# A decoder block in one program: the first 128 tokens go through attention, merge, projections and routing alone, and the second 128 go through them beside the first ones' expert gathers

## The reference

```python
mod = silu(c) @ ada_w + ada_b                    # 1024 x 6144: sh1, sc1, g1, sh2, sc2, g2
h = rms_norm(x, norm1_g) * (1 + sc1) + sh1
z = h @ w_in                                     # q, k, v of both attentions, indexer, gates
# NSA, 8 heads: compressed blocks + selected blocks + window, causal, gated by head
# DSA, 8 heads: the indexer picks 64 keys for each query, then softmax over them
merged = sigmoid(g_nsa) * (o_nsa @ w_br_nsa) + sigmoid(g_dsa) * (o_dsa @ w_br_dsa)
x = x + g1 * (merged @ w_out)
h = rms_norm(x, norm2_g) * (1 + sc2) + sh2
q = (h @ peer_wq).reshape(T, 8, 2, 64)           # routing: 8 heads, two halves each
s_half, i_half = top_k(einsum("thcd,hcnd->thcn", q, subkeys), 16)   # 128 keys a half
top_s, top_p = top_k(sums of the two halves, 16)                    # 16 of 16384 experts
act = gelu(einsum("cd,chkd->chk", h, u[eidx]))   # a row of 1024 of u for each token and pick
x = x + g2 * einsum("chk,chkd->cd", softmax(top_s) * act, v[eidx])  # and one of v
return rms_norm(x, final_g)
```

## Time and profile before

| | |
|---|---|
| median of 3 runs | 1091.7 us |
| the profiled execution's own time | 1091.95 us |
| its span, first to last instruction | 1089.7 us |
| mean granted TensorE clock | 0.915 |
| first gather issued | 406.4 us |
| HBM read over the span | 328.58 MB |

### The profile page before, as it was taken

The page is one execution under the profiler, slowest core; times in us unless marked ns, Lnnn a source line. Parts: engine busy times, 40 slices in busy tenths (PEclk is TensorE's granted clock), DMA queues, the critical chain, the costliest instruction groups (busy, mean ns, idle before and its releaser), DMA issues.

```text
span 1089.7 us, 8493 instructions
## 1 busy us (share of the span) xinstructions
PE 811.3 (74%) x2512; PEld 431.9 (40%) x2512; DVE 632.3 (58%) x1533; ACT 207.2 (19%) x529; POOL 501.2 (46%) x517
## 2 busy tenths in 40 slices
PE   2499889999999860067777777777777777777774
PEld 2344577878888750022222222222222222222221
DVE  4622346679331158998558559459549449545545
ACT  3001132333401240022112112112022022021200
POOL 1000000000000007777777777777777777777472
PEclk8599889986599895579999999999999999999998
DMA  9743304467315009999999999999999999999995
GB/s 340 290 143 100 142 1 149 174 219 252 135 44 208 0 23 381 380 410 409 409 409 409 409 409 409 409 410 409 410 409 409 410 409 410 409 409 410 340 399 215
DMA packets 103470, 330.20 MB, mean 303 GB/s; under 512 B 9025, under 2 KB 11265, under 8 KB 103425
## 3 DMA queue, kind: packets, MB, share of 16 engines
q0 software_dynamic: 73728, 268.47, 62.3%
q1 hardware_dynamic: 29248, 60.73, 15.7%
q10 hardware_dynamic: 448, 0.46, 0.1%
HBM read 328.58 MB, written 1.05 MB: 302 GB/s over the span
## 4 chain that ended last, share of the span: by engine, by line
PE 30%; POOL 27%; DMA 18%; issue 13%; DVE 11%; ACT 1%; DVEq 0%; SPq 0%; POOLq 0%; ACTq 0%
POOL arena L694 14%; POOL extra L683 9%; DMA ring<-in_u,arena 7%; DMA arena<-in_v,arena 7%; PE banks L425 6%; PE banks L500 5%; POOL ring L683 3%; DMA extra<-in_u,arena 3%; PE banks L620 3%; PE banks L596 3%; PE banks L607 3%; PE banks L539 2%; PE banks L574 2%; PE banks L663 1%; PE banks L554 1%
## 5 line engine op out<-in xcount | busy, mean ns | idle before, releaser
L663 PE MATMUL banks<-arena 128*128 128x512 f32 x944 | 461.9, 613 | 215.7 <-DMA arena<-in_v,arena 140.2
L683 POOL DMA_INDIRECT extra<-in_u,arena x192 | 187.4, 976 | 438.1 <-DVE arena L1242 378.1
L663 PEld LDWEIGHTS banks<-arena 128*128 128x128 f32 x944 | 161.5, 190 | 516.1 <-issue 335.0
L1251 DVE CUSTOM_DVE_ANT_0 arena<-extra,banks 128x1024 f32<-128x1024 f32 x192 | 229.0, 1220 | 134.6 <-DMA extra<-in_u,arena 134.2
L694 POOL DMA_INDIRECT arena<-in_v,arena x256 | 247.3, 966 | 88.5 <-issue 62.2
L893 ACT ACTIVATE arena<-tab,arena 128x128 f32<-128x128 f32 x236 | 84.4, 395 | 345.6 <-PE banks L663 275.0
L1251 DVE CUSTOM_DVE_ANT_0 arena<-ring,banks 128x1024 f32<-128x1024 f32 x64 | 77.8, 1221 | 71.0 <-DMA ring<-in_u,arena 70.7
L425 PE MATMUL banks<-arena 128*128 128x512 f32 (+1 forms) x160 | 70.1, 598 | 3.5 <-DVE arena L958 3.5
L683 POOL DMA_INDIRECT ring<-in_u,arena x64 | 61.5, 960 | 19.5 <-issue 16.8
L500 PE MATMUL banks<-arena 128*128 128x256 f32 x256 | 63.3, 403 | 2.4 <-DMA arena<-in_w_gate 2.1
L500 PEld LDWEIGHTS banks<-arena 128*128 128x128 f32 x256 | 50.1, 201 | 12.0 <-DMA arena<-in_w_gate 2.3
(11 more groups left out here) (205 smaller groups left out, 720.9 us busy)
## 6 DMA issues: line engine op xcount, KB each, us to landing
arena<-in_ada_w SPq DMA_DIRECT2D x12, 2048.0 KB, 8.8
arena<-in_w_in SPq DMA_DIRECT2D x4, 2048.0 KB, 7.8
arena<-in_w_gate SPq DMA_DIRECT2D x4, 2048.0 KB, 8.1
arena<-in_w_br SPq DMA_DIRECT2D x2, 2048.0 KB, 8.2
arena<-in_w_out SPq DMA_DIRECT2D x2, 2048.0 KB, 8.5
arena<-in_peer_wq SPq DMA_DIRECT2D x2, 2048.0 KB, 11.0
arena<-in_v,arena POOLq DMA_INDIRECT x256, 12.0
extra<-in_u,arena POOLq DMA_INDIRECT x192, 11.7
```

The costliest lines, as they stand in the source:

```text
L663: last = nc.tensor.matmul(acc[tt][:, half * 512:(half + 1) * 512], diag[i % DIAGS], v_slot[v % VR][:, half * 512:(half + 1) * 512], start= ...
L683: nc.gpsimd.indirect_dma_start(u_slot[g % UR], None, A["u"], bass.IndirectOffsetOnAxis(ap=expert[:, g:g + 1], axis=0)).then_inc(u_in[g % U ...
L1251: V.tensor_tensor_reduce(out=junk[g % 2], in0=u_slot[g % UR], in1=h2row[g // FIRST_HALF][:, :], scale=1.0, scalar=0.0, op0=ALU.mult, op1=A ...
```

## The change

Everything after the compressed branch is split by token tile. Tile 0 goes alone through 12 units, merge, output projection, norm, query projection, sub-key scores and the routing of its first head. Then the step loop begins, and tile 1's units, merge, projections and routing stand at chosen steps of this loop, on every engine's list.

What goes with it:
- Projections have 128 columns instead of 256, and the weights of branches, output and query (six chunks) are loaded twice. Sums 10 and 11 of adaLN, which only the end needs, move into the loop (steps 114 to 129).
- All 12 merge-gate tiles stand in tile 0's 12 units, one each, and the adaLN sums 4 to 9 with four steps of VectorE a unit instead of two or three.
- Weight slots: six (three in `arena`, three in `extra`, where gathered rows go later) for the loads before the gathers, then two in `arena`.
- Gather slots: six for `u` and four for `v` until step 136, then ten and eight, where there were 16 and 8. `LAG` is 22 instead of 40; a block is one head, 16 picks, and its routing is spread over three points of the block before it.
- The dot product writes over its `u` rows, and `h` in rows is copied from PSUM to SBUF, since PSUM is now needed for tile 1's work.

```diff
-WSLOTS = 3
+POST = [(kind, m) for kind in ("br", "out", "wq") for m in range(2)]
+LOADS += [(kind, m, 0) for kind, m in POST]
+EARLY = len(LOADS)
+LOADS += [(kind, m, 1) for kind, m in POST] + [("ada", 10, 0), ("ada", 11, 0)]
+WSLOTS = 6
+SLOT_OF = [n % WSLOTS if n < EARLY else (n - EARLY + 1) % 2 for n in range(len(LOADS))]
-UNITS = [(b, tt, hp) for b in range(3) for tt in range(TT) for hp in range(HEADS // 2)]
+UNITS = [(b, tt, hp) for tt in range(TT) for b in range(3) for hp in range(HEADS // 2)]
-BLOCK = 2 * TOPK
-UR, VR, DIAGS = 16, 8, 16
-LAG = BLOCK + 8
+BLOCK = TOPK
+DIAGS = 8
+LAG = BLOCK + 6
+U_SLOT = [g % 6 if g < 136 else (g - 136) % 10 for g in range(STEPS)]
+V_SLOT = [v % 4 if v < 136 else (v - 136) % 8 for v in range(STEPS)]
+UNIT_AT = {18 + 3 * i: EACH + i for i in range(EACH)}
+AT_OT, AT_BR, AT_OUT, AT_SSQ, AT_WQ, AT_SUB, AT_H2ROW = 55, 57, 74, 91, 94, 111, 112
+AT_X1ROW, AT_ADA, AT_G2ROW, AT_OUT0 = 114, 114, 134, 152
...
+            for g in range(STEPS + LAG):
+                if g + 2 in UNIT_AT:
+                    unit_scores(UNIT_AT[g + 2])
+                if g >= LAG:
+                    if g == LAG + FIRST_HALF:
+                        pe.wait_ge(g2row_out, 1)
+                    if g - LAG in PE_NO:
+                        value_step(g - LAG)
+                if g - 1 in UNIT_AT:
+                    unit_transposes(UNIT_AT[g - 1])
+                if g - 2 in UNIT_AT:
+                    unit_output(UNIT_AT[g - 2])
+                if g == AT_OT:
+                    turn_outputs(1)
+                if AT_BR <= g < AT_BR + 2 * KT and (g - AT_BR) % 2 == 0:
+                    branch(1, (g - AT_BR) // 2)
+                if AT_OUT <= g < AT_OUT + 2 * KT and (g - AT_OUT) % 2 == 0:
+                    mix_out(1, (g - AT_OUT) // 2)
+                if g == AT_SSQ:
+                    square_sum2(1)
+                if AT_WQ <= g < AT_WQ + 2 * KT and (g - AT_WQ) % 2 == 0:
+                    query(1, (g - AT_WQ) // 2)
...
             def u_gather(g):
                 if g % BLOCK == 0:
                     pool.wait_ge(eid_ready, g // BLOCK + 1)
-                if g >= UR:
-                    pool.wait_ge(u_used, g - UR + 1)
+                if U_OLD[g] is not None:
+                    pool.wait_ge(u_used, U_OLD[g] + 1)
...
+            for g in range(STEPS):
+                b, i = divmod(g, BLOCK)
+                if g in UNIT_AT:
+                    unit_mask(UNIT_AT[g])
+                dot(g)
+                if i == 3 and b:
+                    amounts(b - 1)
+                if b + 1 < BLOCKS:
+                    if i == 5:
+                        route_halves(b + 1)
+                    if i == 8:
+                        route_pairs(b + 1)
+                    if i == 11:
+                        route_experts(b + 1)
+                if g - 1 in UNIT_AT:
+                    unit_select(UNIT_AT[g - 1])
```

More of the change, by code:

```diff
@@ L272, in build @@
[L272 to L283, removed]
@@ L286, in build @@
[L286 to L291, removed]
+        product = rope_a
+        x2 = [scr[:, tt * D:(tt + 1) * D] for tt in range(TT)]
@@ new lines, in unit_output @@
+            def unit_output(u):
+                b, tt, hp = UNITS[u]
+                g = u // 4
+                pe.wait_ge(pt_ready, u + 1)
+                if hp == 0:
+                    if g < 2:
+                        pe.wait_ge(oc_read, g + 1)
+                    else:
+                        pe.wait_ge(o_read, g - 1)
+                for i in range(2):
+                    h = 2 * hp + i
+                    for s in range(tt + 1):
+                        if b == 2:
+                            v = kdv[:, s, DH:2 * DH]
+                        else:
+                            first = (2 + b) * P + (h // 4) * DH
+                            v = zv[:, s, first:first + DH]
+                        last = nc.tensor.matmul(o_bank[g][:, h * DH:(h + 1) * DH],
+                                                pT[u % 2][:, (i * (tt + 1) + s) * P:(i * (tt + 1) + s + 1) * P],
+                                                v, start=(s == 0), stop=(s == tt))
+                last.then_inc(o_unit, 1)
@@ new lines, in _ @@
+            ada(9)
+            turn_outputs(0)
+            for m in range(KT):
+                branch(0, m)
+            for m in range(KT):
+                mix_out(0, m)
+            square_sum2(0)
+            for m in range(KT):
+                query(0, m)
+            key_scores(0)
+            rows(BB[1], h2, 0).then_inc(h2row_done, 1)
+            pe.wait_ge(sub_ready, 4)
+            for g in range(STEPS + LAG):
[20 more added lines that the diff above has]
+                    query(1, (g - AT_WQ) // 2)
+                if g == AT_SUB:
+                    key_scores(1)
+                if g == AT_H2ROW:
+                    rows(BB[2], h2, 1).then_inc(h2row_done, 1)
+                if g == AT_X1ROW:
+                    pe.wait_ge(sub_ready, 8)
+                    for tt in range(TT):
+                        rows(BB[tt], x3, tt).then_inc(x1row_done, 1)
+                if g == AT_G2ROW - 3:
+                    ada(10)
+                    ada(11)
+                if g == AT_G2ROW:
+                    pe.wait_ge(g2diag_ready, KT)
+                    pe.wait_ge(x1row_out, 1)
+                    for half in range(2):
+                        last = nc.tensor.matmul(B[half][:, :], ones[:, :], g2diag[:, half * 512:(half + 1) * 512],
+                                                start=True, stop=True)
+                    last.then_inc(g2row_done, 1)
@@ L1192, in best16 @@
             def best16(srcs, values, indices, works, before):
[L1196 to L1197 removed]
+                each = range(len(srcs))
+                done = [mark(V.max(values[i][:, 0:8], srcs[i])) for i in each]
                 dve.wait_ge(dve_step, before)
[L1199 removed]
+                for i in each:
                     dve.wait_ge(dve_step, done[i])
```

726 lines of the change are left out of this document (398 added, 328 removed).

## The result

The changed kernel takes 1088.4 us in the median (20 runs, 1078.8 to 1101.9); the kernel before, run beside it, 1091.6 us (20 runs, 1089.5 to 1096.1). The ratio is 0.995, with an interval of 0.993 to 0.997: 3 us faster, where 34 were forecast (1058 us). The ratio goes by the 16 runs within 1.5% of the fastest; the other four took 1095.9 to 1101.9 us. The profiled execution took 1088.85 us, its span is 1087.0.

The account below looks back on a forecast made before the run. The prediction took DMA, at 409 GB/s or 1.283 us a gather, as the bound, with GpSimd close behind. Its terms were 310 + 38 + 347 + 341 + 20 + 2.2 = 1058 us, range 1022 to 1098.

Parts of the forecast that it names:

- The first gather: End of the work ahead of the gathers: first gather at 310 us, bounds 300 and 351, 96 us earlier.
- the 244 of the sum: Opening and tile 0's units: branch projections start at 171 + 73 = 244 us, before at 292.39.
- the rival built on it: Projections: weight loads lie end to end with matmuls, half the columns do not halve them; 1117 at most, chance 0.04.
- Steps 0 to 21: First-table gathers only, into six slots: 38 us, where DMA alone would need 28.
- Steps 22 to 134: Gathers beside the second tile's work: 3.1 us a step, 112 x 3.1 = 347 us.
- bursts of TensorE: Mixed stretch, steps 22 to 134: TensorE bursts empty the DMA queue; 29 us above the DMA floor.
- The loads' 31 us: Mixed stretch: six weight loads of 2.1 MB cost DMA 6 x 5.13 = 31 us.
- From step 134 on: Ten and eight slots, nothing else beside, DMA sets it: 266 gathers x 1.283 = 341 us.
- The last landing and the tail: End of the kernel: a last landing of about 8 us and 12 of final norm and store, 20 us.
- DMA stays full: Rival: mixed stretch at 2.84 us a step, 318 for 347; 1029 us, or 1020 without the ramp; chance 0.23.
- The four value slots decide: Rival: delayed value matmuls stall GpSimd and DMA runs dry; 3.6 us a step, 403 for 347, 1114 us; chance 0.09.
- the third: Rival that half the columns do not halve the projections: 1058 + 37 + 22 = 1117 at most; chance 0.04.

Follow-up runs that it names:

- the sixth experiment: The kernel after with all dots of both tiles reading h from PSUM, tile 1's units on single score and transpose banks; 1039.0 us, ratio 0.9528.
- the eighth: The sixth experiment with tile 1's output projection and what follows it three steps later; 1033.3 us, ratio 0.9468.
- the seventh: The sixth experiment with the six late weight loads cut to an eighth of their bytes, the work on them kept; 1009.5 us, ratio 0.9245.
- the first experiment: The kernel after with the second tile's dots (tokens 128 to 255) reading h from PSUM; 1056.4 us, ratio 0.9675.
- fourth experiment: The first experiment with six u and four v slots to the end, not ten and eight after step 136; 1074.1 us, ratio 0.9841.
- fifth: The first experiment with tile 0's dots also reading h from PSUM from step 60 on; 1054.0 us, ratio 0.9652.
- the second experiment: The kernel before with h copied to SBUF and the dots reading it there, nothing else changed; 1158.1 us, ratio 1.0634.
- experiment 1152: Not a label: 1152 is the lowest time in us of the second experiment, the kernel before with h copied to SBUF; median 1158.1 us.
- experiment 1037: Not a label: 1037 is the lowest time in us of the sixth experiment, the kernel after with all dots reading h from PSUM; median 1039.0 us.

## Why the prediction was wrong

- **The first gather** was forecast at 310 us and came at 302.7 (302.3 to 307.9 over the executions with this opening). Of the 7 us, 5 lie before the branch projections, which begin at 238.84 for the 244 of the sum. The three projections took 17.36, 14.53 and 14.96 us for 16 each, so half the columns do halve them; the chain of waits of the kernel after:

```profile
238.84 17.36 PE banks L618 x128
257.58 14.53 PE banks L629 x128
276.25 14.96 PE banks L648 x128
```

  The rule of the Trainium skill that was weighed there (TensorE: Matmul & The Clock Gate, Part 3), and the rival built on it, fall for these matmuls: 0.136 us an instruction in the first, at a granted clock of 0.83, and 0.113 and 0.117 in the others, at 1.00, not 0.21.
- **Steps 0 to 21**: 38 us forecast, 39.4 measured.
- **Steps 22 to 134**: 347 us forecast, 352.6 measured. The size was right and the reason only partly. Above the DMA floor of 318 (2.84 a step) lie 34.6 us. The sixth experiment takes away 20.8 by lifting the hold on GpSimd, which stood nowhere in the prediction; the eighth takes 3.6, the late output weights; 10 are left, where the forecast had put 29 for bursts of TensorE, and no run takes them apart. The loads' 31 us are borne out by the seventh.
- **From step 134 on, the step that failed.** The prediction put it: 266 gathers x 1.283 = 341 us at 409 GB/s, "nothing else beside", "DMA sets it". Measured: 694.7 to 1068.6, 373.9 us, 1.405 a gather. What replaced the bound is GpSimd: 1.12 for an issue and 0.30 behind it. Of the prediction's signs this is the one that failed: 369 GB/s from 700 on, not 409, while the rate from the first gather to 695 us was 360, inside the 350 to 390 that it named. With `h` in PSUM for these dots alone (the first experiment) the same stretch takes 344 us and the kernel 1056.4 us, 2 off the forecast of 1058.
- **The last landing and the tail**: 20 us forecast from the last issue, 18.5 measured.
- **The rivals.** None of them named the hold. "DMA stays full" (1020 to 1029) is what the eighth kernel nearly does, at 1033. "The four value slots decide" is not seen in the steady part (fourth experiment). The top of the third, 1117, takes 37 us for the three projections where the ends named, 16 and 29.7, give 3 x 13.7 = 41; nothing hangs on it.

The price was to be had from the trace of before. The copy of `h` to SBUF stands in the list of what the change does, and the prediction gave it no price: it kept 1.23 us for a dot, which holds, and asked nothing more. It had read GpSimd at 2.48 of 2.56 us a step and wrote that it "cannot win back a stall", but did not ask what stalls it. The trace of before has the stall, where VectorE reads two long operands from SBUF, in the routing's comparisons:

```profile
576.24 1.96 DVE L1238 TENSOR_TENSOR arena<-tab,arena 128x1728 f32<-128x1728 f32 x1
576.81 2.20 POOL L694 DMA_INDIRECT arena<-in_v,arena  x1 [0.30 <-issue]
578.23 1.96 DVE L1240 TENSOR_TENSOR arena<-arena 128x1728 f32<-128x1728 f32 x1
579.31 1.69 POOL L683 DMA_INDIRECT extra<-in_u,arena  x1 [0.30 <-issue]
...
580.22 1.95 DVE L1241 TENSOR_REDUCE arena<-arena 128x32 f32<-128x1728 f32 x1
...
581.31 0.94 POOL L694 DMA_INDIRECT arena<-in_v,arena  x1 [0.30 <-issue]
```

576.24 + 1.96 + 0.81 = 579.01 = 576.81 + 2.20, and the second pair comes out alike. The third is not held: the sum L1241 is as long, and reads one input. So it is all through this trace: of the issues that begin during L1238 or L1240 all 14 are held, of those during L1241 none of 7, and of the 201 that begin in a dot early enough for a hold to show, none; those dots have one input in PSUM. From the first two pairs the price can be worked out. An issue that begins s after the start of a dot of 1.23 is held until 2.04, which is 1.10 - s longer than 0.94; falling anywhere in a step of 2.57 it loses 1.10 x 1.10 / 2 / 2.57 = 0.24 on average, two issues 0.47, and 2.48 + 0.47 = 2.95 a step is over the 2.57 that DMA needs. As an estimate that is 133 x 2.95 = 392 us for this part, where 374 were measured (0.16 an issue; they fall less often into a dot than by chance).

The Trainium skill has a rule that bears on it (SBUF — State Buffer, "Who interferes with whom"): a VectorE operation with both inputs in SBUF contends with GpSimd's reads, and the order of issue decides who blocks. The trace agrees on the first. On the second it agrees for the issue that comes second, which is held; a dot that comes second is not held (80 issues, dots of 1.23). The same section names `tensor_tensor` as an operation that did not stall DMA; for these gathers, whose indices GpSimd takes from SBUF, the trace says otherwise.

Two inputs in SBUF may not be the only case. In four kernels (the first, fifth, sixth and seventh experiments) one issue each begins 0.21 to 0.23 us after the adaLN product that has a single tensor input in SBUF and runs through 512 columns in 0.48 us, and takes 1.06 to 1.08; the same rule gives 1.06 to 1.08. (Those that begin within 0.07 us of its start take 0.94.) Four issues are few, and no run was made for it. From the sixth:

```profile
660.44 0.49 DVE L1088 TENSOR_SCALAR ring<-arena,silu 128x512 f32<-128x512 f32 x1
660.67 1.06 POOL L777 DMA_INDIRECT extra<-in_u,arena  x1 [0.60 <-DVE arena L1421]
```

Two things stay open. What in an issue is held is not shown: that its last 0.81 us come after the VectorE operation fits a read of the indices near its start, but no kernel here moves the indices. And the kernels with the hold on every dot vary more (the kernel after 1079 to 1102 in 20 runs, the second experiment 1152 to 1168 in six) than those without it (before 1090 to 1096 in 20, the sixth experiment 1037 to 1044 in five), which would fit holds that depend on how the engines' phases fall; that was only argued.

## What to carry to other kernels

When a buffer moves from PSUM to SBUF, ask who else works while it is read: here it cost the reader nothing, and the engine that issues the gathers 0.16 us each, 49 us in the kernel after and 67 in the kernel before. Where an engine has 3% of slack in its period, look in the trace of before for its longest instructions of a kind, and for what runs beside them: that is the price of every further such neighbour. And price weight loads beside a full DMA by their bytes, since they hide behind nothing.

## What the runs showed of the hardware

- A gather's issue on GpSimd (0.94 us) that begins during a VectorE instruction with two long inputs in SBUF ends 0.81 us after it, or 0.94 after its own start if that is later; one that begins earlier is not held, and the dot keeps its 1.23 us (1.28 at most). With one of the dot's inputs in PSUM there is no hold (0 of 201), and none beside a sum over 1728 columns with one input (0 of 7).
- A 128x128 float32 weight with 128 columns costs 0.113 to 0.117 us an instruction at a granted clock of 1.00, in runs of 128, about half of the 0.218 with 256 columns at the same clock.
- The 2 MB loads of output weights beside the gathers landed in 22 us in the median, against 11 for those ahead of them (two loads each); six such loads took from the gathers about what their bytes cost (29 us measured, 27 by bytes).
